# Two state-space groups in one block of a hybrid transformer kernel

## The chip, the cores and the metric

The kernel runs on one core of one Trainium2 chip. The metric is the device time of one execution in microseconds (us); the median of several runs counts. A core has five engines with their own instruction queues: TensorE (PE; its weight loads are shown apart as PEld), VectorE (DVE), ScalarE (ACT), GpSimd (POOL) and SyncE (SP), which here only starts transfers. Engines wait for each other by semaphores. TensorE writes its products to PSUM, which has eight banks of 128x512 fp32; everything else lives in SBUF. TensorE's clock has two levels, 1.2 and 2.4 GHz; the profile gives the granted clock as a share of 2.4 GHz, and "cold" and "warm" below mean the lower and the higher one.

## What is computed

A block with a hybrid mixer and a mixture of experts, then two more layers with attention. The change touches the state-space (SSD) part of the first mixer: 16 heads of width 64 in two groups of 8, for 512 tokens in both directions. For one direction of one group:

```python
c = silu(centred_dwconv(n @ w_in, conv_w, conv_b))     # B, C, x of the group; z is a gate
cs = cumsum(dt * A)                                    # per head, within a chunk
Lmat = exp(cs_i - cs_j), j <= i
y_intra = ((C_i . B_j) * Lmat) @ (x * dt)
chunk_states = B^T @ (x * dt * exp(cs_last - cs))
h = h * exp(cs_last) + chunk_states                    # carried from chunk to chunk
y = y_intra + (C @ h) * exp(cs)
y = (y_fw + y_bw + D * x) * silu(z)
y = rms_norm(y over the 512 channels of the group)
```

The kernel uses chunks of 128 tokens, four of them.

## The kernel before

The program is a row of stages. `stage` (line 63) opens a block in which each engine has its own instruction list, and ends it with a barrier of all engines that also clears the semaphores. Activations lie with channels on the 128 partitions and the 512 tokens in the free dimension, so a "tile" is 128 channels x 512 tokens. All products are fp32.

The mixer first normalizes its input to `m.xT` (8 tiles), then runs one long stage `gdn` (line 754) for the other kind of heads, four pairs of them. That stage also projects and convolves the ten tiles of SSD group 0 at its end (`ssd_order`): tiles 0 and 1 are B and C, 2 to 5 are x, 6 to 9 the gates z. Then `ssd_group` (line 1252) is called for g = 0 and 1. For group 1 it begins with the stage of `mixer_tiles` (line 661): five slabs of weights (1 MB each, four buffers of `m.ring`), ten tiles of 8 multiplications each (`product`, line 104), six of them through the seven taps of `convolve` (lines 650 and 654 on VectorE, two tiles in turns) and a SiLU on ScalarE (line 702), four directly through a SiLU (line 705). The other four stages run for each group:

- `ssd_tokens` (line 1280): TensorE transposes B and the x tiles (1287) and multiplies C with B (1290); VectorE scales the transposed x by step sizes into `x_in` and `x_out` (1306) and masks the C-B product (1310).
- `ssd_states` (line 1313): six multiplications (1321), and on VectorE the carried states (1333, 1336, 1339).
- `ssd_heads` (line 1342): 16 combinations of head pair j, head hh and direction d. GpSimd lays out `gu` (1352, two buffers), TensorE makes two 128x512 products of it (1364, 1365) in banks 0 to 3, ScalarE takes their exponentials (1396) into `c_dec` and `score`, and VectorE multiplies these with C (1413) and with the masked C-B (1416). Combination n waits until the exponentials of n - 2 have freed its banks. After each four combinations TensorE makes an output tile of 28 short products (1385), which VectorE adds to D x (1405) and multiplies with the gate (1409).
- `ssd_norm` (line 1422): squares on ScalarE (1430), four products with ones (1438), mean, root (1432), reciprocal (1447) and four products with the gain (1449).

So the two groups take nine stages. Nothing of group 1 starts before group 0 is done. The part behind it, `down_stage`, multiplies with `w_out`.

## Time and profile before

| | us |
|---|---|
| median of 3 runs (3831.04 to 3834.41) | 3832.28 |
| profiled execution | 3832.88 |
| its span | 3831.0 |
| TensorE busy in the span | 3380.7 |
| VectorE / ScalarE / GpSimd busy | 1742.8 / 1030.6 / 246.7 |
| mean granted clock | 0.937 |
| the state-space stages, first transposes of group 0 to last product of norm 1 | 768.2 to 1023.8 |

The page gives sums over the whole program, of which the state-space stages are 7%. To read them one needs the timeline of each engine in 767 to 1024 us, and the busy times by stretch. In a row of the timeline the first number is the start, the second the time from the first start to the last end of the merged instructions (an instruction's own time overlaps the next a little), "x16" their count, and the bracket the idle time of the engine before it and what ended it. "PEq L67" is the barrier.

### The profile page before, as it was taken

Reading aid. Unit: us, or ns where it says so; the run is one execution under the profiler, and the core shown is the slowest. Engines: PE = TensorE matmul, PEld = TensorE weight load, DVE = VectorE, ACT = ScalarE, POOL = GpSimd, SP = SyncE. Lnnn points to the kernel's source line nnn. Section 1 sums busy time; section 2 is a strip of 40 time slices with the busy share of each in tenths; the row PEclk is TensorE's granted clock in tenths of the full one; section 3 lists DMA queues with packets and bytes.
Section 4 is the critical chain, followed back from the end, with each engine's and each line's share of the span. In section 5 each row is a group of like instructions: output and inputs, shape, how many; then the busy total and the mean of one; then the engine's idle time right before and its main releaser. Section 6 shows DMA issues by size and latency. Waiting matters only on the chain. (4 is left out here: it accounts for less than half of the span.)

```text
span 3831.0 us, 39352 instructions
## 1 busy us (share of the span) xinstructions
PE 3380.7 (88%) x15418; PEld 2434.6 (64%) x15418; DVE 1742.8 (45%) x2515; ACT 1030.6 (27%) x1467; POOL 246.7 (6%) x212
## 2 busy tenths in 40 slices
PE   4988899868877775999998889998999998889997
PEld 3464765633465223788784557887888784468886
DVE  2757676664533002543235645432543326644433
ACT  2121211220321002322213443222322213543222
POOL 1100100020210001000002000000000002000001
PEclk6999999979887998999998899999999999899998
DMA  2100010001212992322211013221322211013221
GB/s 76 56 34 34 12 45 33 1 12 44 77 58 87 420 420 94 121 99 95 89 69 61 1 45 121 99 97 63 117 91 95 102 52 61 1 66 110 99 99 55
DMA packets 50693, 326.33 MB, mean 85 GB/s; under 512 B 7041, under 2 KB 7425, under 8 KB 13057
## 3 DMA queue, kind: packets, MB, share of 16 engines
q1 hardware_dynamic: 50560, 324.52, 22.7%
q8 instruction: 89, 1.46, 0.2%
q14 instruction: 44, 0.35, 0.0%
HBM read 321.35 MB, written 2.10 MB: 84 GB/s over the span
## 5 line engine op out<-in xcount | busy, mean ns | idle before, releaser
L364 PE MATMUL psum<-ffn_x_hi,ffn_w_hi 128*128 128x512 f32 x1408 | 548.8, 390 | 1.1 <-DVE ffn_x_lo L320 1.0
L364 PE MATMUL psum<-ffn_x_lo,ffn_w_hi 128*128 128x512 f32 x1408 | 547.8, 389 | 0.0
L364 PE MATMUL psum<-ffn_x_hi,ffn_w_lo 128*128 128x512 f32 x1408 | 547.8, 389 | 0.0
L309 DVE TENSOR_TENSOR ffn_w_lo<-ffn_raw,ffn_w_hi 128x2048 fp32r<-128x2048 f32 x128 | 293.4, 2292 | 420.6 <-ACT ffn_w_hi L280 420.6
L104 PE MATMUL psum<-mix_normed,mix_ring 128*128 128x512 f32 x832 | 378.9, 618 | 51.3 <-DVE recurrences_work L654 21.5
L280 ACT ACTIVATE ffn_w_hi<-ffn_raw 128x2048 fp32r<-128x2048 f32 x128 | 245.2, 1916 | 566.9 <-PE psum L364 566.8
L104 PEld LDWEIGHTS psum<-mix_normed,mix_ring 128*128 128x128 f32 x832 | 164.1, 199 | 262.6 <-issue 238.5
L364 PEld LDWEIGHTS psum<-ffn_x_hi,ffn_w_hi 128*128 128x128 f32 x1408 | 264.6, 188 | 61.1 <-DVE ffn_w_lo L316 6.5
L364 PEld LDWEIGHTS psum<-ffn_x_lo,ffn_w_hi 128*128 128x128 f32 x1408 | 264.7, 188 | 55.0
L364 PEld LDWEIGHTS psum<-ffn_x_hi,ffn_w_lo 128*128 128x128 f32 x1408 | 264.3, 188 | 54.9
L364 PE MATMUL psum<-ffn_hid_hi,ffn_w_hi 128*128 (+1 forms) x704 | 273.9, 389 | 0.0
L364 PE MATMUL psum<-ffn_hid_lo,ffn_w_hi 128*128 (+1 forms) x704 | 273.9, 389 | 0.0
L364 PE MATMUL psum<-ffn_hid_hi,ffn_w_lo 128*128 (+1 forms) x704 | 273.9, 389 | 0.0
L335 DVE TENSOR_TENSOR ffn_lift<-psum,squares_sb 128x512 f32<-128x512 f32 x88 | 60.8, 691 | 309.8 <-PE psum L364 309.8
L364 PEld LDWEIGHTS psum<-ffn_hid_hi,ffn_w_hi 128*128 128x128 f32 x704 | 132.1, 188 | 27.5
L364 PEld LDWEIGHTS psum<-ffn_hid_lo,ffn_w_hi 128*128 128x128 f32 x704 | 132.1, 188 | 27.4
L364 PEld LDWEIGHTS psum<-ffn_hid_hi,ffn_w_lo 128*128 128x128 f32 x704 | 132.1, 188 | 27.4
L654 DVE SCALAR_TENSOR_TENSOR recurrences_work<-psum,mix_group_cols,recurrences_work 128x509 f32<-128x509 f32 (+2 forms) x216 | 143.3, 745 | 0.0
L172 POOL TENSOR_TENSOR squares_sb<-squares_sb,ffn_gates 128x512 f32<-128x512 f32 x28 | 35.9, 1283 | 1451.4 <-ACT ffn_gates L162 1447.9
L298 ACT ACTIVATE ffn_hid_hi<-ffn_lift 128x512 f32 (+1 forms) x88 | 55.6, 632 | 267.7 <-DVE ffn_lift L339 267.7
L416 PE MATMUL psum<-mix_out_s_hi,mix_out_w_hi 128*128 128x512 f32 x256 | 101.0, 395 | 7.1 <-DVE mix_out_w_lo L473 7.1
L172 POOL TENSOR_TENSOR squares_sb<-squares_sb,mix_norm_tmp 128x512 f32<-128x512 f32 x42 | 53.6, 1276 | 826.1 <-ACT mix_norm_tmp L162 820.9
(454 smaller groups left out, 5323.3 us busy)
## 6 DMA issues: line engine op xcount, KB each, us to landing
ffn_raw<-w_ffn SPq DMA_DIRECT2D x128, 1024.0 KB, 4.7
mix_ring<-w_experts SPq DMA_DIRECT2D x48, 1024.0 KB, 13.6
mix_ring<-w_mix SPq DMA_DIRECT2D x32, 1024.0 KB, 7.0
mix_normed<-w_experts SPq DMA_DIRECT2D x24, 1024.0 KB, 13.6
experts_slabs<-w_experts SPq DMA_DIRECT2D x24, 1024.0 KB, 13.6
mix_ring<-w_gdn SPq DMA_DIRECT2D x16, 1024.0 KB, 4.8
mix_ring<-w_ssd SPq DMA_DIRECT2D x10, 1024.0 KB, 4.8
mix_ring<-w_out SPq DMA_DIRECT2D x7, 1024.0 KB, 7.1
```

Source lines behind the costliest of these rows:

```text
L104: ins = pe.matmul(out, weights(k), moving(k), start=(k == 0), stop=(k == n - 1))
L172: pool.tensor_tensor(m.squares, m.squares, tmp[:, k % 2, :], ALU.add).then_inc(folded, 1)
L280: act.activation(w_hi[:, q, :], raw[:, q, :], ACT.Copy).then_inc(hi_done, 1)
L298: act.activation(hid_hi[:, n, :], lift, ACT.Copy).then_inc(hid_hi_done, 1)
L309: dve.tensor_tensor(w_lo[:, q, :], raw[:, q, :], w_hi[:, q, :].bitcast(F32), ALU.subtract)\
L335: dve.tensor_tensor(lift, m.ps[:, 2 * q + 1, :], rstd, ALU.mult).then_inc(taken, 1)
L364: ins = pe.matmul(out, wp[:, q, w], xp, start=start and a == 0, stop=stop and a == 2)
L416: pe.matmul(out, a[0], b[0], start=start, stop=False)
L654: ins = dve.scalar_tensor_tensor(d[:, lo:hi], s[:, lo + shift:hi + shift], col[:, tap:tap + 1], d[:, lo:hi], ALU.mult, ALU.add)
```

## The change

`ssd_group`, `mixer_tiles` and the loop over the groups give way to one function `ssd_groups` with one stage for both groups. Each engine's list is now one written order:

- SyncE asks for the five slabs of group 1 at the start, into two buffers (the second half of the ring); slab s waits until the tiles of s - 2 are projected.
- TensorE puts the tiles of group 1 in pairs (`tiles(s)`, in the order 6, 7, 0, 1, 2, 3, 4, 5, 8, 9, in banks 6 and 7) between the steps of group 0, and the tokens, states and norm sums of either group between heads.
- VectorE convolves a pair (`conv`) between the products of the heads of group 0; ScalarE's SiLUs stand between its exponentials.
- Norm 0's squares, sums, mean, root and products stand among the heads of group 1.
- Buffers move: group 1 has its own tiles `c[1]`, its columns are in `m.cur_buf`, `score[0]` is where `x_out` was, the squares replace the gates, and `y` replaces the x tiles. Banks are given out by `token_banks` and `state_banks`.

The computation and the number of products are the same.

The core of the diff:

```diff
-        return [cut(m.work, (6 + i) * T, T) for i in range(4)]
+        return [m.mixed[:, KD + 6 + i, :] for i in range(2)] + [cut(m.rope_tables, i * T, T) for i in range(2)]
...
-def ssd_group(nc, m, io, g):
+def ssd_groups(nc, m, io):
...
-        mixer_tiles(nc, m, f"ssd_project_{g}", io["w_ssd"], g, io["ssd_cols"][g], 6, 4, c, gate)
+    scal = lambda n, g: m.scal[n][:, :, :, (0 if n == "step_to_end" else GH) + 8 * g:][:, :, :, 0:8]
+    combos = [(j, hh, d) for j in range(4) for hh in range(2) for d in range(2)]
...
+    place = {n: at for at, n in enumerate(order)}
+    tile_bank = lambda n: m.ps[:, 6 + place[n] % 2, :]
+    token_banks = ((0, 1, 2, 3, 4, 5), (4, 5, 6, 7, 4, 5))
+    state_banks = ((0, 1, 2, 3, 4, 5), (6, 7, 4, 5, 6, 7))
+    flat = lambda a: a.rearrange("p t i -> p (t i)")
...
-    with stage(nc, m, f"ssd_tokens_{g}") as (block, sem):
...
+    with stage(nc, m, "ssd") as (block, sem):
...
+        @block.sync
+        def _(sp):
+            sp.dma_start(cols[1], io["ssd_cols"][1]).then_inc(cols_in, 16)
+            for s in range(len(order) // 2):
+                if s >= 2:
+                    sp.wait_ge(projected, 2 * (s - 1))
+                sp.dma_start(slab(s).rearrange("p k n -> p (k n)"),
+                             io["w_ssd"][len(order) // 2 + order[2 * s] // 2]).then_inc(landed[s % 2], 16)
+
...
+            def tiles(s):
+                pe.wait_ge(landed[s % 2], 16 * (s // 2 + 1))
+                for at in (2 * s, 2 * s + 1):
+                    if s == 1:
+                        pe.wait_ge(silued, at - 1)
+                    elif s:
+                        pe.wait_ge(steps, 14 * (s - 1))
+                    product(pe, m.ps[:, 6 + at % 2, :], lambda k: slab(s)[:, k, at % 2 * P:at % 2 * P + P],
+                            lambda k: m.xT[:, k, :]).then_inc(projected, 1)
...
+            def tokens(g):
+                banks = token_banks[g]
+                if g:
+                    pe.wait_ge(y_read, 4)
+                    pe.wait_ge(silued, len(order))
+                for p, n in enumerate((0, 2, 3, 4, 5)):
...
-    with stage(nc, m, f"ssd_states_{g}") as (block, sem):
...
-    with stage(nc, m, f"ssd_heads_{g}") as (block, sem):
...
-    with stage(nc, m, f"ssd_norm_{g}") as (block, sem):
...
+            def fresh_states(g):
+                pe.wait_ge(b_copied, g + 1)
+                pe.wait_ge(taken, 4 * g + 4)
+                pe.wait_ge(cross_read, g + 1)
...
+                            pe.wait_ge(state_done, 6 + at - 3)
+                        pe.matmul(m.ps[:, state_banks[g][at], :], b_tok[:, t, :], x_out[:, d, t, :], start=True,
+                                  stop=True).then_inc(fresh, 1)
...
+            def decay(g, n):
+                d, at = n % 2, 16 * g + n
+                pe.wait_ge(laid, at + 1)
+                if at >= 2:
+                    pe.wait_ge(decayed, 2 * (at - 1))
+                else:
+                    pe.wait_ge(state_done, 6)
+                pe.matmul(m.ps[:, 2 * (n % 2), :], m.ones, flat(gu[:, n % 2, :, :]), start=True, stop=True)\
+                    .then_inc(decays, 1)
+                pe.matmul(m.ps[:, 2 * (n % 2) + 1, :], after[d], flat(gu[:, n % 2, :, :]), start=True, stop=True)\
+                    .then_inc(decays, 1)
+
+            def outputs(g, i):
+                if 4 * g + i >= 2:
+                    pe.wait_ge(y_read, 4 * g + i - 1)
+                if i < 2:
+                    pe.wait_ge(state_done, 6 * g + 6)
+                pe.wait_ge(scored, 32 * g + 2 * (4 * i + 4))
...
+            def sums(g):
+                if g == 0:
+                    pe.wait_ge(state_done, 11)
+                for i in range(4):
+                    pe.wait_ge(squared, 4 * g + i + 1)
+                    ins = pe.matmul(m.ps[:, 6, :], m.ones, gate[g][i], start=(i == 0), stop=(i == 3))
+                ins.then_inc(summed, 1)
+
+            tokens(0)
+            tiles(0)
+            fresh_states(0)
+            tiles(1)
+            for n in range(4):
+                decay(0, n)
+            for j in range(1, 5):
+                for n in range(4 * j, 4 * j + 4) if j < 4 else ():
+                    decay(0, n)
+                if j < 4:
+                    tiles(j + 1)
+                outputs(0, j - 1)
+            decay(1, 0)
+            decay(1, 1)
+            tokens(1)
+            decay(1, 2)
+            decay(1, 3)
+            fresh_states(1)
+            sums(0)
+            for j in range(1, 5):
+                for n in range(4 * j, 4 * j + 4) if j < 4 else ():
+                    decay(1, n)
+                outputs(1, j - 1)
+            sums(1)
...
+            def silu(n):
+                act.wait_ge(projected, place[n] + 1)
+                if n < 6:
+                    act.wait_ge(steps, 14 * (n // 2 + 1))
+                    act.activation(c[1][:, n, :], c[1][:, n, :], ACT.Silu).then_inc(silued, 1)
+                else:
+                    act.activation(gate[1][n - 6], tile_bank(n), ACT.Silu).then_inc(silued, 1)
...
+            def exps(g, ns):
+                for n in ns:
+                    if n >= 8:
+                        act.wait_ge(y_done, 4 * g + n // 4 - 1)
+                    elif g:
+                        act.wait_ge(y_done, 3 + n // 4)
+                    for half, dst in ((0, c_dec), (1, score[g])):
+                        act.wait_ge(decays, 32 * g + 2 * n + half + 1)
+                        act.activation(dst[:, n % 8, :], m.ps[:, 2 * (n % 2) + half, :], ACT.Exp).then_inc(decayed, 1)
...
+            copy_b(0)
+            for n in (6, 7, 0, 1):
+                silu(n)
+            exps(0, range(0, 8))
+            for n in (2, 3):
+                silu(n)
+            exps(0, range(8, 12))
+            for n in (4, 5):
+                silu(n)
+            exps(0, range(12, 16))
+            for n in (8, 9):
+                silu(n)
+            exps(1, range(0, 2))
+            copy_b(1)
+            squares(0)
+            exps(1, range(2, 8))
+            root(0)
+            exps(1, range(8, 16))
+            squares(1)
+            root(1)
...
+            def conv(a):
+                two = (a, a + 1)
+                if a == 0:
+                    dve.wait_ge(cols_in, 16)
+                convolve(dve, m, [tile_bank(n) for n in two], [c[1][:, n, :] for n in two],
+                         [cols[1][:, 8 * n:8 * n + 8] for n in two], projected, [place[n] + 1 for n in two], steps,
+                         7 * a)
+
...
+            tokens(0)
+            carry(0)
+            conv(0)
+            scores(0, range(0, 8))
+            conv(2)
+            out(0, 0)
+            scores(0, range(8, 12))
+            conv(4)
+            out(0, 1)
+            scores(0, range(12, 16))
+            out(0, 2)
+            out(0, 3)
+            tokens(1)
+            carry(1)
+            scores(1, range(0, 4))
+            average(0)
+            scores(1, range(4, 8))
+            normed(0)
+            out(1, 0)
+            scores(1, range(8, 12))
+            out(1, 1)
+            scores(1, range(12, 16))
+            out(1, 2)
+            out(1, 3)
+            average(1)
+            normed(1)
 
 
 
@@ -3034,8 +3110,7 @@
                     resid_norm_stage(nc, m, "norm1", m.gains["norm1"], m.xT)
                     scalars_stage(nc, m, io)
                     gdn_heads(nc, m, io)
-                    for g in range(SG):
-                        ssd_group(nc, m, io, g)
+                    ssd_groups(nc, m, io)
                 down_stage(nc, m, "mix1_out", io["w_out_1"], 0, m.mixed, 2 * KD, 1.0)
             resid_norm_stage(nc, m, "norm2", m.gains["norm2"], m.xT)
             with expert_memory(nc, m):
```

What moves on TensorE, at the start of the state-space part. Line 1287 (now 1280) are the transposes, 1321 (1298) the state products, 104 the projection tiles; branches stand where a stage ends. Before:

```order
L1287 MATMUL psum<-const_sb,recurrences_work 128x128 x20
L1290 MATMUL psum<-recurrences_work 128x128 x4
L65 UNCONDITIONAL_BRANCH
L1316 UNCONDITIONAL_BRANCH
L1321 MATMUL psum<-recurrences_work 128x512 x6
L65 UNCONDITIONAL_BRANCH
L1355 UNCONDITIONAL_BRANCH
```

After:

```order
L1259 UNCONDITIONAL_BRANCH
L1280 MATMUL psum<-const_sb,recurrences_work 128x128 x20
L1285 MATMUL psum<-recurrences_work 128x128 x4
L104 MATMUL psum<-mix_normed,mix_ring 128x512 x16
L1298 MATMUL psum<-recurrences_work 128x512 x6
L104 MATMUL psum<-mix_normed,mix_ring 128x512 x16
L1308 MATMUL psum<-mix_norm_tmp,const_sb 128x512
L1310 MATMUL psum<-mix_norm_tmp,const_sb 128x512
```

Two pairs of tiles of group 1 now stand ahead of and behind the state products, and no stage ends between them.

What moves on ScalarE, in the heads of group 0 (line 1396, now 1392, are the exponentials; 1296/1374 the copy of B; 702/1380 SiLUs of convolved tiles and 705/1382 of gates; 1430 and 1432 belong to norm 0). Before:

```order
L1296 ACTIVATE recurrences_work<-psum 128x512
L65 UNCONDITIONAL_BRANCH
L1389 UNCONDITIONAL_BRANCH
L1396 ACT_TABLE_LOAD
L1396 ACTIVATE mix_ring<-psum 128x512 x32
L65 UNCONDITIONAL_BRANCH
L1427 UNCONDITIONAL_BRANCH
L1430 ACTIVATE mix_ring<-recurrences_work 128x512 x4
L1432 ACT_TABLE_LOAD
```

After (the two exponentials of combination 0 are shown, of the 16 ahead of the next SiLU):

```order
L1374 ACTIVATE recurrences_work<-psum 128x512
L1382 ACT_TABLE_LOAD
L1382 ACTIVATE mix_mixed<-psum 128x512 x2
L1380 ACTIVATE recurrences_work<-recurrences_work 128x512 x2
L1392 ACT_TABLE_LOAD
L1392 ACTIVATE mix_ring<-psum 128x512
L1392 ACTIVATE recurrences_work<-psum 128x512
```

The SiLUs of four tiles of group 1 now stand ahead of the first exponential of group 0, and table loads come between SiLUs and exponentials.

## Rows read from the trace of the kernel before

**Rows 1.** The head of the page: span and instruction count.

```profile
span 3831.0 us, 39352 instructions
```

**Rows 2.** Stretches: length, busy us of PE, PEld, DVE, ACT, POOL; PEclk, DMA share, GB/s.

```profile
857.00:935.00 78.00, 71.93 (x160) 31.40 (x160) 28.30 (x42) 6.64 (x11) 0.00 (x0) 0.92 0.18 68
...
767.00:1024.00 257.00, 197.61 (x832) 100.56 (x832) 150.61 (x191) 57.18 (x91) 39.38 (x32) 0.85 0.05 21
```

**Rows 3.** Timeline (start us, us, engine, line, operation [idle before]): where norm 0 ends and projection 1 starts.

```profile
853.85 2.74 DVE L1449 SCALAR_TENSOR_TENSOR mix_mixed<-recurrences_work,mix_group_cols,mix_norm_tmp 128x512 f32<-128x512 f32 x4
...
857.50 1.28 ACT L702 ACT_TABLE_LOAD   x1 [7.08 <-PEq L67]
...
857.87 22.28 SPq L675 DMA_DIRECT2D mix_ring<-w_ssd  x5
...
862.79 71.93 PE L104 MATMUL psum<-mix_normed,mix_ring 128*128 128x512 f32 x160 [13.76 <-DMA mix_ring<-w_ssd]
```

**Rows 4.** Timeline, TensorE, state-space stages (a 128x512 f32 multiplication is two records).

```profile
768.21 4.50 PE L1287 MATMUL psum<-const_sb,recurrences_work 128*128 128x128 f32 x20 [11.25 <-PEq L67]
...
782.00 7.84 PE L1321 MATMUL psum<-recurrences_work 128*128 128x512 f32 x12 [8.06 <-PEq L67]
...
804.95 1.02 PE L1364 MATMUL psum<-mix_norm_tmp,const_sb 128*128 128x512 f32 x2
...
812.07 3.28 PE L1385 MATMUL psum<-mix_ring,recurrences_work 128*64 128x128 f32 x56
...
842.36 6.68 PE L1438 MATMUL psum<-mix_ring,const_sb 128*128 128x512 f32 x8 [3.14 <-ACT mix_ring L1430]
...
936.30 2.38 PE L1287 MATMUL psum<-const_sb,recurrences_work 128*128 128x128 f32 x20 [1.58 <-PEq L67]
```

**Rows 5.** Timeline, VectorE, state-space stages.

```profile
770.19 9.66 DVE L1306 TENSOR_TENSOR recurrences_work<-psum,mix_scalars 128x512 f32<-128x512 f32 x16 [2.96 <-PE psum L1287]
...
779.76 1.28 DVE L1310 TENSOR_TENSOR recurrences_work<-psum,const_sb 128x512 f32<-128x512 f32 x2
...
803.55 1.53 DVE L1413 TENSOR_TENSOR mix_ring<-mix_ring,recurrences_work 128x512 f32<-128x512 f32 x1
...
815.89 0.73 DVE L1405 SCALAR_TENSOR_TENSOR recurrences_work<-recurrences_work,mix_group_cols,psum 128x512 f32<-128x512 f32 x1
...
840.05 0.69 DVE L1409 TENSOR_TENSOR recurrences_work<-recurrences_work,mix_mixed 128x512 f32<-128x512 f32 x1
...
850.46 3.35 DVE L1447 RECIPROCAL mix_norm_tmp<-mix_norm_tmp 128x512 f32<-128x512 f32 x1 [0.69 <-ACT mix_norm_tmp L1432]
...
893.57 0.81 DVE L650 TENSOR_SCALAR recurrences_work<-psum,mix_group_cols 128x512 f32<-128x512 f32 x1 [4.33 <-PE psum L104]
...
907.30 0.81 DVE L650 TENSOR_SCALAR recurrences_work<-psum,mix_group_cols 128x512 f32<-128x512 f32 x1 [4.33 <-PE psum L104]
...
908.02 7.96 DVE L654 SCALAR_TENSOR_TENSOR recurrences_work<-psum,mix_group_cols,recurrences_work 128x509 f32<-128x509 f32 x12
...
1021.09 2.74 DVE L1449 SCALAR_TENSOR_TENSOR mix_mixed<-recurrences_work,mix_group_cols,mix_norm_tmp 128x512 f32<-128x512 f32 x4
```

**Rows 6.** Timeline, ScalarE: an exponential, a table load and what follows it.

```profile
699.52 1.28 ACT L973 ACT_TABLE_LOAD   x1
...
700.82 1.15 ACT L973 ACTIVATE mix_mixed<-mix_mixed 128x512 f32<-128x512 f32 x2
...
797.52 0.60 ACT L1396 ACTIVATE mix_ring<-psum 128x512 f32<-128x512 f32 x1 [1.95 <-PE psum L1364]
```

**Rows 7.** Timeline, GpSimd: one cumulative decay tile.

```profile
803.47 1.06 POOL L1352 TENSOR_TENSOR mix_norm_tmp<-const_sb,mix_scalars 128x512 f32<-128x512 f32 x1 [0.39 <-PE psum L1365]
```

**Rows 8.** TensorE after idle time: a timeline row, then stretches as in rows 2.

```profile
681.89 16.98 PE L104 MATMUL psum<-mix_normed,mix_ring 128*128 128x512 f32 x32 [3.47 <-DVE recurrences_work L654]
...
795.00:800.00 5.00, 4.59 (x6) 2.01 (x7) 0.83 (x2) 1.76 (x3) 2.09 (x3) 0.50 0.00 2
...
800.00:805.00 5.00, 5.00 (x13) 2.04 (x12) 4.23 (x4) 2.98 (x5) 2.70 (x3) 0.94 0.00 0
```

292 lines of the change are left out of this document (111 added, 181 removed).

## The prediction

> **What bounds the kernel now.** I read the busy time by stretch first. The state-space part runs from 767 to 1024 us of a span of 3831.0 us [rows 1, 2]. TensorE is busy 197.61 of these 257 us, more than any other engine, but at a mean granted clock of 0.85 of the full 2.4 GHz: part of its busy time is the same work at 1.2 instead of 2.4 GHz. So the part is a chain that goes through TensorE, with stops at the stage ends. I then read the timeline at one such end. The last product of norm 0 ends at 853.85 + 2.74 = 856.59, the next stage's first instruction starts at 857.50, so a barrier costs 0.9 us. Behind it the first weight slab is asked for at 857.87, and TensorE starts at 862.79, 4.9 us later, after 13.76 us idle [rows 3]. All of projection 1 (71.93 us of TensorE) stands alone: VectorE is busy 28.30 of 78 us there [rows 2, 3]. The token and norm stages are the opposite: VectorE or a short chain works, and TensorE waits.
>
> **Times of the parts.** Twenty transposes take 2.38 us warm and 4.50 us cold [rows 4]. Two projection tiles of 8 multiplications took 907.30 - 893.57 = 13.73 us [rows 5], so one 128x512 multiplication takes 0.86 us warm, and a cold one 1.7 (6.68 us for four, [rows 4]). A combination (head, direction) has two of them, 1.72 us. An output tile takes 3.28 less overlap, 3.2. On VectorE the scaling of the tokens and the C-B product take 9.66 + 1.28 - overlap = 10.9 us, a convolution of two tiles 0.7 + 7.96 = 8.7 us after the second tile is there [rows 5]. On ScalarE two SiLUs take about 1.15, a table load 1.28, an exponential 0.60 [rows 6].
>
> **The walk after the change.** It starts at the same point, 768.2 [rows 4]; all before it is unchanged.
> (1) Transposes and cross products of group 0 as before, to 774.0. The first slab is now asked for at the same barrier and needs the same 4.9 us, to about 773: hidden. The next two tiles end at 787.8. Group 0's scaling on VectorE (until 781.0, [rows 5]) lies under them.
> (2) Six state multiplications 5.1, then tiles 3 and 4 13.7: 806.6. The carried states are under those tiles.
> (3) Here is the new wait. Combinations 0 and 1 fill the two pairs of PSUM banks, until 810.0. Combination 2 needs the exponentials of 0, and on ScalarE these stand behind the SiLUs of tiles 0 and 1 (the order of ScalarE above, lines 1380 and 1392), which need the convolution of both. Convolution 0.2 + 8.7, SiLUs 1.2, table 1.3, two exponentials 1.2: 12.5 us after the tile pair, 819.1. TensorE idles 9.1 us.
> (4) Six combinations 10.3, two tiles 13.7: 843.1. After such an idle stretch the clock is low: after 3.47 us idle, 32 records (two tiles) took 16.98 us where 13.73 is warm [rows 5, 8]. After the states ended at 782.00 + 7.84 = 789.8, TensorE came back at about 795.4 (busy 4.59 of the stretch 795 to 800), ran at 0.50 there and at 0.94 in the next 5 us [rows 4, 8]. That is 2.3 (half of 4.6) to 3.2 us each; I take 2.7. Sum 845.8.
> (5) Then twice the same period from tile pair to tile pair: 12.5 to the freed banks (outputs of 3.2 and two combinations of 3.4 fill it up to a gap of 5.8 us), two combinations 3.4, cold clock 2.7, tiles 13.7, together 32.3: 878.1 and 910.4.
> (6) Two output tiles 6.4, combinations 0 and 1 of group 1 3.4, the transposes up to VectorE's first tile 1.9, its scaling 10.9 (combinations 2 and 3 under it): 933.0. TensorE has been idle 4 us.
> (7) Six state multiplications 5.1 + 2.7 cold, waiting for the carried states 0.7, sums of norm 0 3.4: 944.9.
> (8) From combination 4 to the last gating before: 804.95 to 840.05 + 0.69 = 840.74, 35.8 us. VectorE sets the pace there: it takes eight combinations from 798.1 (797.52 + 0.60, [rows 6]) to 815.89, 2.2 us each against TensorE's 1.72; one of its two products is stretched to 1.53 us while GpSimd makes a decay tile [rows 5, 7]. So norm 0's work there (0.69 mean, 3.35 reciprocal, 2.74 products) adds up to 6.8 [rows 5], at least 0 if it fills holes. I take 5.9, near the upper end since that engine is the late one: 986.6.
> (9) The last norm: square 0.6, one sum multiplication (three are done already) 1.7, mean 0.7, root 0.7, reciprocal 3.4, products 2.7, handovers 0.3: 996.7. Before, this tail took 856.59 - 840.74 = 15.9 in group 0.
>
> Before, the same place is 1021.09 + 2.74 = 1023.8 [rows 5]. The gain is 27.1 us by this sum. Handovers of 0.05 to 0.2 us between engines, some ten more on the chain than I listed, take back about 1: **26 us**. The profiled execution took 3832.88 us, 1.88 around its span, and the median is 0.6 lower. 3832.3 - 26 gives **3806 us** (the like of 3806.9 for a profiled one).
>
> Two edits cost nothing. The barriers: eight are gone, about 7.5 us, already in the walk since it has none. The slab loads: two buffers instead of four, but a slab has 25 us and more between its uses and takes 4.9.
>
> A rule that speaks against the change. A table load is 1.28 us, and the next ScalarE instruction starts 0.02 us behind it (699.52 + 1.28 = 700.80, then 700.82) [rows 6]. The new order of the two groups has 11 loads where 5 stood, but only the three of steps 3 to 5 are on the chain. The Trainium skill, "ScalarE: Activation LUTs", section "Table sets: the hidden batching unit", says to do all functions of one set before switching, and "What ACT_TABLE_LOAD costs" gives 2.66 us a switch, since a drain comes on top. By that the three would cost 4.1 us more, and the result would be 3810. The rows show no such drain.
>
> **The rivals.**
> - Clock holds. If gaps of 4 to 6 us did not lower the clock, and that of 9 did not either, 4 x 2.7 = 10.8 us fall out: 3795. Rows 8 speak against it.
> - GpSimd stretches the convolutions too. While conv runs, TensorE consumes two decay tiles, so GpSimd makes two more; products with both inputs in SBUF were stretched by 1.53 - 0.69 = 0.84 [rows 5, 7]. No convolution of before runs beside GpSimd, so the bounds are 0 and 3 x 2 x 0.84 = 5.0 us: 3811. I take 0, because a convolution step has its main input in PSUM like the scaling steps, and only one in SBUF. The Trainium skill, "SBUF — State Buffer", section "Who interferes with whom", has the same condition: only a VectorE instruction with two SBUF inputs contends with a GpSimd one that reads SBUF. By that it is 0.
> - A switch of ScalarE costs as much again on the chain. By the nearest row, one more 1.28 us for each of the three: 3.8, so 3810. Rows 6, with 0.02 us behind a load, speak against it. This is the rule above.
> - The overlap doesn't come: the idle stretches are as long as what was hidden, and only barriers (7.5) and the wait for the slab (5.3) are saved: 3819.
> - Slower. If TensorE stayed at the low clock through the interleaved stretch (819 to 921), its 82 us of warm work there (three tile pairs 41, 16 combinations 27, four outputs 13) would grow. It turns slower where over 26 us of it, a third, run cold beyond the short restarts; wholly cold gives 3870. The gaps are 6 us in 32, and before, the clock was back at 0.94 within 5 us [rows 8], so 0.02.
>
> **How the numbers follow.** Forecast 0.70 (3801 to 3811), clock holds 0.08, GpSimd 0.07, drains 0.05, no overlap 0.06, within 0.2% of before 0.02, slower 0.02. A measurement can tell about 0.2%, 7.7 us, from no change. The range 3797 to 3816 takes in the forecast with its own bounds (step 4: 0.5 a gap; step 8: +0.9, -5.9), GpSimd and drains; it leaves out most of "clock holds", "no overlap" and the last two, 0.18. Faster 0.96, same 0.02, slower 0.02.
>
> **What would show it.** In the timeline of TensorE after the change: idle stretches of about 9, 6 and 6 us before combinations 2, 10 and 14 of group 0, each ended by a ScalarE exponential, and a clock of 0.5 behind them; transposes of group 1 near 921; the last product near 997. Twelve convolution steps in 8.0 us as before would rule out GpSimd's lock, a gap above 0.1 us between a load and its activation would show the drain. I am wrong above all if the stretch from combination 4 of group 1 isn't paced by VectorE, or if the gaps in step 5 are longer than 5.8 us.

## The result and the profile after

| | before | after |
|---|---|---|
| median of 4 runs, us | 3833.17 (3831.04 to 3834.41) | 3801.95 (3796.39 to 3804.26) |
| profiled execution / its span | 3832.88 / 3831.0 | 3804.26 / 3802.2 |
| state-space part, first transposes to last product of norm 1 | 768.21 to 1023.83: 255.6 | 772.78 to 999.00: 226.2 |

The ratio is 0.9918 (95% interval 0.9906 to 0.993): 31.2 us faster, against a forecast of 26 us (3806, range 3797 to 3816).

Outside the state-space part nothing changed: the rest of the span is 3831.0 - 255.6 = 3575.4 us before and 3802.2 - 226.2 = 3576.0 after. Over all kernels shown below this rest lies between 3567 and 3580 us from one profiled execution to the next, although its code is the same, so a difference of a few us is read from the length of the part, not from medians. The part itself repeats: a second profile of the changed kernel, in another set of runs, gave 226.2 us again.

The head of the page of the changed kernel, and the stretch that holds the part (length, busy us of PE, PEld, DVE, ACT, POOL, PEclk, DMA share, GB/s), answering [rows 1, 2]:

```profile
span 3802.2 us, 39200 instructions
...
772.00:1000.00 228.00, 188.17 (x833) 97.35 (x833) 139.92 (x190) 63.33 (x98) 37.56 (x32) 0.91 0.07 24
```

TensorE is busy 188.17 of 228 us at a mean clock of 0.91, where it was 197.61 of 257 at 0.85. The work is the same; its busy time is shorter because less of it runs cold.

TensorE's timeline after the change, answering [rows 3, 4]:

```profile
772.78 4.50 PE L1280 MATMUL psum<-const_sb,recurrences_work 128*128 128x128 f32 x20 [11.26 <-PEq L67]
778.71 14.00 PE L104 MATMUL psum<-mix_normed,mix_ring 128*128 128x512 f32 x32 [0.25 <-DMA mix_ring<-w_ssd]
...
792.54 5.31 PE L1298 MATMUL psum<-recurrences_work 128*128 128x512 f32 x12
797.69 13.90 PE L104 MATMUL psum<-mix_normed,mix_ring 128*128 128x512 f32 x32
811.43 1.02 PE L1308 MATMUL psum<-mix_norm_tmp,const_sb 128*128 128x512 f32 x2
...
824.10 2.05 PE L1308 MATMUL psum<-mix_norm_tmp,const_sb 128*128 128x512 f32 x2 [9.08 <-ACT recurrences_work L1392]
825.94 1.91 PE L1310 MATMUL psum<-mix_norm_tmp,const_sb 128*128 128x512 f32 x2
...
836.97 13.90 PE L104 MATMUL psum<-mix_normed,mix_ring 128*128 128x512 f32 x32
...
864.66 2.05 PE L1308 MATMUL psum<-mix_norm_tmp,const_sb 128*128 128x512 f32 x2 [6.95 <-ACT recurrences_work L1392]
...
870.77 13.90 PE L104 MATMUL psum<-mix_normed,mix_ring 128*128 128x512 f32 x32
...
898.46 2.04 PE L1308 MATMUL psum<-mix_norm_tmp,const_sb 128*128 128x512 f32 x2 [6.96 <-ACT recurrences_work L1392]
...
904.74 13.90 PE L104 MATMUL psum<-mix_normed,mix_ring 128*128 128x512 f32 x32
...
940.44 7.08 PE L1298 MATMUL psum<-recurrences_work 128*128 128x512 f32 x12 [3.87 <-DVE recurrences_work L1440]
...
951.81 1.02 PE L1308 MATMUL psum<-mix_norm_tmp,const_sb 128*128 128x512 f32 x2
...
984.54 3.28 PE L1331 MATMUL psum<-mix_ring,recurrences_work 128*64 128x128 f32 x56 [1.39 <-DVE mix_ring L1478]
```

The 13.76 us of idle time before the projection [rows 3] are 0.25 us now. In their place stand three idle stretches, 9.08, 6.95 and 6.96 us, each ended by a ScalarE exponential, and behind each of them products that take 2.05 and 1.91 us instead of 1.02. The state products of group 1, behind a wait of 3.87 us, run partly cold as well (7.08 us, where group 0's take 5.31). The clock rows behind the first of the three stretches show the lower of the two levels, 1.2 GHz, and then the way up (columns as above):

```profile
824.00:826.00 2.00, 1.90 (x3) 0.89 (x4) 2.00 (x4) 0.94 (x2) 0.00 (x0) 0.50 0.03 8
...
828.00:830.00 2.00, 2.00 (x4) 0.72 (x3) 1.02 (x2) 1.09 (x2) 0.98 (x1) 0.76 0.00 0
```

What ScalarE does before the first two of these stretches end (1382 and 1380 are SiLUs, 1392 exponentials):

```profile
774.52 1.28 ACT L1382 ACT_TABLE_LOAD   x1
...
820.41 1.15 ACT L1380 ACTIVATE recurrences_work<-recurrences_work 128x512 f32<-128x512 f32 x2 [27.07 <-DVE recurrences_work L654]
821.58 1.28 ACT L1392 ACT_TABLE_LOAD   x1
822.87 0.60 ACT L1392 ACTIVATE mix_ring<-psum 128x512 f32<-128x512 f32 x1
...
859.67 1.28 ACT L1380 ACT_TABLE_LOAD   x1 [21.91 <-DVE recurrences_work L654]
860.97 1.15 ACT L1380 ACTIVATE recurrences_work<-recurrences_work 128x512 f32<-128x512 f32 x2
862.13 1.28 ACT L1392 ACT_TABLE_LOAD   x1
863.43 0.60 ACT L1392 ACTIVATE mix_ring<-psum 128x512 f32<-128x512 f32 x1
```

TensorE has filled the two pairs of PSUM banks that the exponentials are to free, and ScalarE waits for the convolution of the next two tiles, because in its list their SiLUs stand first. In the second stretch there are two table loads in the chain, not one: the load for the SiLU starts only when the convolution is done. A load doesn't always wait for the work behind it. The first one, at 774.52, ran at once, and its SiLU waited for its tile until 785.88. The list has one wait in front of that SiLU, and two in front of those of line 1380. In this profile the loads ahead of a single wait that lasted (774.52, 905.55, 990.01) all ran ahead of it, and the loads that stood behind an idle stretch (859.67, 893.48, 926.03, 963.37) all belong to activations with two. No run changes this alone.

VectorE and GpSimd beside each other, a convolution with two decay tiles, and at the end the norms (VectorE rows 1495 and 1498):

```profile
812.36 7.96 DVE L654 SCALAR_TENSOR_TENSOR recurrences_work<-psum,mix_group_scalars,recurrences_work 128x509 f32<-128x509 f32 x12
...
813.39 1.05 POOL L1256 TENSOR_TENSOR mix_norm_tmp<-const_sb,mix_scalars 128x512 f32<-128x512 f32 x1 [38.57 <-PE psum L1310]
815.11 1.05 POOL L1256 TENSOR_TENSOR mix_norm_tmp<-const_sb,mix_scalars 128x512 f32<-128x512 f32 x1 [0.67 <-PE psum L1310]
...
962.51 3.34 DVE L1495 RECIPROCAL const_sb<-const_sb 128x512 f32<-128x512 f32 x1
965.88 4.32 DVE L1498 SCALAR_TENSOR_TENSOR mix_mixed<-recurrences_work,mix_group_cols,const_sb 128x512 f32<-128x512 f32 x4
...
988.63 0.69 DVE L1487 TENSOR_TENSOR recurrences_work<-recurrences_work,const_sb 128x512 f32<-128x512 f32 x1
...
996.26 2.74 DVE L1498 SCALAR_TENSOR_TENSOR mix_mixed<-recurrences_work,mix_group_scalars,const_sb 128x512 f32<-128x512 f32 x4
```

### The profile page after: what moved, and what is told of

It is laid out like the page before. It is cut to its first block and busy times, and to the rows that moved or that the text cites. A ratio compares the mean times of both kernels' runs of the same rounds, so it can differ in the third digit from the quotient of the medians.

```text
span 3802.2 us, 39200 instructions
## 1 busy us (share of the span) xinstructions
PE 3369.6 (89%) x15418; PEld 2427.8 (64%) x15418; DVE 1732.8 (46%) x2515; ACT 1037.4 (27%) x1473; POOL 244.7 (6%) x212
## 5 line engine op out<-in xcount | busy, mean ns | idle before, releaser
L172 POOL TENSOR_TENSOR squares_sb<-squares_sb,ffn_gates 128x512 f32<-128x512 f32 x28 | 35.9, 1282 | 1450.0 <-ACT ffn_gates L162 1446.6
L654 DVE SCALAR_TENSOR_TENSOR recurrences_work<-psum,mix_group_cols,recurrences_work 128x510 f32<-128x510 f32 (+2 forms) x180 | 119.4, 741 | 0.0
```

Source lines behind the costliest of these rows:

```text
L172: pool.tensor_tensor(m.squares, m.squares, tmp[:, k % 2, :], ALU.add).then_inc(folded, 1)
L654: ins = dve.scalar_tensor_tensor(d[:, lo:hi], s[:, lo + shift:hi + shift], col[:, tap:tap + 1], d[:, lo:hi], ALU.mult, ALU.add)
```

## The experiments

Each was compared with the kernel before on its own chip, whose medians there were 3831.14, 3831.51, 3832.03 and 3829.4 us. Line numbers in the diffs' kernels are those of the changed kernel, shifted by a few lines where code was added.

**Again.** The changed kernel itself.

> The changed kernel once more, beside the others of this set. It should come within 0.2% of its first median, 3802 us, and the state-space part (first transposes to last product of norm 1) should again take 226.2 us, since nothing in it depends on chance but the clock. If the 29.4 us of that part in the first profile were partly luck of the clock, the part would take 229 or more here.

Measured: 3799.77 us (3797.5 to 3802.73), ratio 0.9918 (0.9903 to 0.9934), part 226.2 us, as expected. It serves as the point of comparison below.

**Exponentials first.** Only ScalarE's list is reordered, so that each pair of SiLUs stands behind the exponentials that TensorE waits for.

```diff
-            for n in (6, 7, 0, 1):
+            for n in (6, 7):
                 silu(n)
             exps(0, range(0, 8))
-            for n in (2, 3):
+            for n in (0, 1):
                 silu(n)
             exps(0, range(8, 12))
-            for n in (4, 5):
+            for n in (2, 3):
                 silu(n)
             exps(0, range(12, 16))
-            for n in (8, 9):
+            for n in (4, 5, 8, 9):
                 silu(n)
```

> The changed kernel with ScalarE's list in another order: each batch of exponentials of group 0 stands ahead of the SiLUs of the tile pair in front of which TensorE waited (exponentials 0 to 7, then SiLUs 0 and 1, and so on). Nothing else is changed. Theory 'gaps': the three idle stretches of TensorE (9.1, 7.0 and 7.0 us) are due only to this order, so they go, and the cold restarts behind them (2.5 to 2.7 us each) go too: 23 + 8 = 31 us less, about 3771 us, part about 196 us. Rival 'VectorE takes over': the products wait for the same VectorE that convolves, so the gaps come back as waits for scored products, and no more than 10 us are gained: 3792 us or more.

Measured: 3777.75 us (3774.88 to 3784.16), ratio 0.9865 (0.985 to 0.988), part 204.8 us: 21.4 less, two thirds of the 31 us that theory 'gaps' expected and far more than the 10 of its rival. The three idle stretches are gone. But a new one of 6.60 us stands in the first group's heads. TensorE's row, then GpSimd's, then the first and the last of twelve VectorE products:

```profile
823.29 2.07 PE L1308 MATMUL psum<-mix_norm_tmp,const_sb 128*128 128x512 f32 x2 [6.60 <-POOL mix_norm_tmp L1256]
...
815.06 9.18 POOL L1256 TENSOR_TENSOR mix_norm_tmp<-const_sb,mix_scalars 128x512 f32<-128x512 f32 x2 [0.67 <-PE psum L1310]
...
815.04 0.68 DVE L1475 TENSOR_TENSOR mix_ring<-mix_ring,recurrences_work 128x512 f32<-128x512 f32 x1
...
821.66 0.68 DVE L1478 TENSOR_TENSOR recurrences_work<-recurrences_work 128x512 f32<-128x512 f32 x1
```

Two decay tiles took 9.18 us instead of 2.1. VectorE's products stand 0.60 us apart from 815.04 to 822.34, none of them stretched, and TensorE goes on 0.95 us behind the last of them, which is about one tile (1.05). So GpSimd was shut out for the whole run. The sum closes to 0.3 us: the three stretches are 23.0 us and their cold restarts 7.7 ("clock kept" below), less 6.60 and 1.9 for the new one (2.07 + 1.88 - 2.04) makes 22.2. The state products of group 1 were slower here, 8.46 us instead of 7.08, and from their start to the norm sums it took 1.1 us more, which leaves 21.1 against the measured 21.4.

The same happened once more in this run, for a shorter time, in the heads of group 1. GpSimd's row, then TensorE's:

```profile
948.30 4.06 POOL L1256 TENSOR_TENSOR mix_norm_tmp<-const_sb,mix_scalars 128x512 f32<-128x512 f32 x2 [3.67 <-PE psum L1310]
...
950.96 1.12 PE L1308 MATMUL psum<-mix_norm_tmp,const_sb 128*128 128x512 f32 x2 [1.02 <-POOL mix_norm_tmp L1256]
```

The first of these two tiles began 0.18 us behind the sixth of eight VectorE products (948.12). That one and the next two took their usual 0.68 us, and TensorE waited 1.02 us for the tile. In the changed kernel the tile at the same place, 974.78, began 0.18 us behind the sixth product too (974.60), and there it got its turn after that product: it took 1.40 us, and the next product was stretched to 1.53.

**Serial.** One block as in the change, but the projection isn't interleaved: group 0's heads, then ten tiles in a row through all eight banks, then group 1. Norm 0 still stands among the heads of group 1. All of ScalarE's exponentials of group 0 stand ahead of its SiLUs, all of VectorE's scores ahead of its convolutions.

```diff
-    order = (6, 7, 0, 1, 2, 3, 4, 5, 8, 9)
+    order = tuple(range(10))
...
-    tile_bank = lambda n: m.ps[:, 6 + place[n] % 2, :]
+    tile_bank = lambda n: m.ps[:, place[n] % 8, :]
...
-            tiles(0)
             fresh_states(0)
-            tiles(1)
...
-                if j < 4:
-                    tiles(j + 1)
                 outputs(0, j - 1)
+            for s in range(5):
+                tiles(s)
+            pe.wait_ge(silued, len(order))
```

> One block without barriers, but with no interleaving: group 0's heads are finished first, then the ten tiles of group 1 run in one row through eight PSUM banks, as before the change, then group 1. Theory 'gaps': interleaving in the written order pays for what it hides (23 us idle and 8 us cold clock against some 20 us of hidden token and state work); the gain of the change comes from the eight barriers (7.5), the wait for the first slab (5.3), the hidden norm 0 (12 to 16) and fewer cold restarts. Then this kernel is no slower than the changed one: the part takes 213 to 226 us, 3787 to 3802 us. Rival 'overlap': the projection beside the heads is what gains, and without it only barriers and slab wait remain: 3815 to 3819 us.

Measured: 3788.35 us (3778.89 to 3793.13), ratio 0.9886 (0.9871 to 0.99), part 209.5 us: 46.1 less than before and 16.7 less than the interleaved change, and even below the 213 to 226 of theory 'gaps'. TensorE's states of group 0, and the ten tiles:

```profile
785.18 8.19 PE L1300 MATMUL psum<-recurrences_work 128*128 128x512 f32 x12 [7.30 <-DVE recurrences_work L1433]
...
836.89 68.93 PE L104 MATMUL psum<-mix_normed,mix_ring 128*128 128x512 f32 x160
```

The tiles run warm without a stop, 68.93 us where the stage of before took 71.93 and had a wait of 6.2 ahead of it (862.79 - 856.59, [rows 3]). So the gain of the change doesn't come from hiding the projection. It comes from the single block with norm 0 in it, and the interleaving of the projection, in the order in which ScalarE's list has it, loses 16.7 us of that again. In the better order of "exponentials first" it gains 4.7 (204.8 against 209.5). By pieces, from rows of before and of this run: up to the first projection tile 64.7 us instead of 72.5 up to the last gating (7.8), norm 0 off the path (15.9), projection 68.9 instead of 79.7 up to the transposes of group 1 (10.8), and group 1 75.9 instead of 87.5 (11.6); together 46.1. These are differences of rows; no run takes out one of them alone.

**Two barriers.** The kernel before, with a second bare barrier at the end of each of the nine state-space stages.

```diff
+    if name.startswith('ssd_'):
+        nc.all_engine_barrier()
```

> The kernel before with a second barrier of all engines behind each of its nine state-space stages. Theory 'barrier is 0.9 us': 9 x 0.8 to 1.0 = 7 to 9 us more, about 3841 us. Rival 'a barrier also costs clock': the longer idle times lower TensorE's clock where it now holds, up to 2.7 us for some of them: 3845 to 3855 us.

Measured: 3831.69 us (3823.92 to 3841.23, 11 runs), ratio 1.0003 (0.9994 to 1.0013). No difference, where 3841 us or more was expected. TensorE's wait ahead of the states, which was 8.06 [rows 4]:

```profile
781.74 7.67 PE L1323 MATMUL psum<-recurrences_work 128*128 128x512 f32 x12 [8.40 <-PEq L69]
```

It grew by 0.34 us, and the like waits of group 1 by 0.33 (9.97 against 9.64, 1.91 against 1.58). A bare barrier behind another one thus costs a third of the 0.9 us that passed at a stage end [rows 3]. The rest of the 0.9 (branches, the clearing of semaphores, the wait for each engine's last instruction) wasn't taken apart. Nine times 0.33 is 3.0 us, less than the runs can tell. In this profile the part was even 2.2 us shorter than in that of before, 253.4, mainly because the sums of norm 1 took 3.70 us where [rows 4] has 6.68 for the like of norm 0: a cold or warm restart at one and the same place differs between executions.

**Clock kept.** The change, with 10, 7 and 7 multiplications on constants in the three idle stretches, into banks that are free there (VectorE's reading of an output tile is waited for before the last). Each takes 0.87 us warm (two records).

```diff
-            for n in range(4):
-                decay(0, n)
+            decay(0, 0)
+            decay(0, 1)
+            keep_running(pe, m, m.ps[:, 4, :], 10)
+            decay(0, 2)
+            decay(0, 3)
...
+                    if n in (10, 14):
+                        if n == 14:
+                            pe.wait_ge(y_read, 1)
+                        keep_running(pe, m, m.ps[:, 5 if n == 10 else 4, :], 7)
```

> The changed kernel with idle work in TensorE's three gaps: 10, 7 and 7 multiplications with no use, into a bank that is free, ahead of combinations 2, 10 and 14 of group 0 (8.6, 6.0 and 6.0 us in gaps of 9.08, 6.95 and 6.96). Theory 'the gap is paid twice': the restart behind each gap is cold and costs 2.3 to 2.9 us more, and the work keeps the clock, so the part shrinks from 226.2 by 7 to 8 us, to about 219; median about 3793. Rival: the clock is not what makes the first combinations behind a gap slow (ScalarE and VectorE pace them, the banks come free late): no change, 226.

Measured: 3790.91 us (3788.46 to 3791.32), ratio 0.9892 (0.9875 to 0.9908), part 219.2 us. The first stretch now, filled with 20 records, and the product behind it:

```profile
809.08 8.75 PE L111 MATMUL psum<-const_sb 128*128 128x512 f32 x20
818.32 1.10 PE L1308 MATMUL psum<-mix_norm_tmp,const_sb 128*128 128x512 f32 x2 [0.50 <-ACT recurrences_work L1399]
...
828.83 13.90 PE L104 MATMUL psum<-mix_normed,mix_ring 128*128 128x512 f32 x32
...
926.92 8.33 PE L1298 MATMUL psum<-recurrences_work 128*128 128x512 f32 x12 [3.87 <-DVE recurrences_work L1447]
```

The product takes 1.10 us and not 2.05. The part is 226.2 - 219.2 = 7.0 us shorter, as the theory has it, and the stretches themselves remain: ScalarE is as late as before. The price of each restart is read from the rows, from the first product behind the stretch to the next tile pair: 828.83 - 818.32 = 10.51 us, where the change has 836.97 - 824.10 = 12.87, so 2.4 us; at the other two stretches 3.51 us each, where the change has 6.11 and 6.28, so 2.6 and 2.8. Together that is 7.7. Of this 1.1 was lost again at the state products of group 1, which take 8.33 us here and 7.08 in the change, behind the same wait of 3.87 us (the granted clock is 0.50 from their start here; in the change it is 0.90 for their first 2 us and 0.50 only after that), and 0.4 was gained at the first tiles, which didn't wait for their slab here.

**Without norm 0 on VectorE.** Its mean (1491) stays, and so does the root on ScalarE.

```diff
-                dve.wait_ge(inverted, g + 1)
+                dve.wait_ge(inverted, 1)
...
-            normed(0)
+            dve.wait_ge(rooted, 1)
```

> The changed kernel without VectorE's reciprocal and four products of norm 0 (6.1 us of work, 7.6 as they ran beside GpSimd); the output of these four tiles is left out. My sum gave 5.9 us to norm 0 among the heads of group 1, since VectorE was to be the late engine there: then the part falls to 220.5. Rival 'it fills holes': the only wait for a VectorE product there is 1.39 us, in front of the last output tile, so the part falls by about 1.4, to 224.8.

Measured: 3798.0 us (3790.76 to 3806.19), ratio 0.9903 (0.9886 to 0.9921), part 224.5 us: only 1.7 less, as the rival has it. From combination 4 to the last gating the time is 35.9 us (950.94 to 986.81), with norm 0 37.5 (951.81 to 989.32). VectorE's rows where norm 0 was:

```profile
961.63 0.73 DVE L1484 SCALAR_TENSOR_TENSOR recurrences_work<-recurrences_work,mix_group_scalars,psum 128x512 f32<-128x512 f32 x1
962.40 0.69 DVE L1487 TENSOR_TENSOR recurrences_work<-recurrences_work,mix_mixed 128x512 f32<-128x512 f32 x1
964.41 0.69 DVE L1475 TENSOR_TENSOR mix_ring<-mix_ring,recurrences_work 128x512 f32<-128x512 f32 x1 [1.32 <-ACT mix_ring L1392]
```

VectorE comes to the output tile at once and then waits 1.32 us for ScalarE's exponentials; behind that, more of its products meet a decay tile and are stretched. Its waits from there to the last gating add up to 5.1 us, and to 2.1 with norm 0. So the five instructions, 7.7 us as they ran beside GpSimd (3.34 + 4.32), mostly filled time in which VectorE would have waited, or in which its products would have been stretched. The price of the whole norm 0 wasn't measured: the wait of 1.32 us holds a table load of ScalarE (962.49, 1.28 us) which the root makes necessary, and which this version keeps.

**GpSimd let in.** "Exponentials first", and VectorE waits before the products of combination n until GpSimd has laid three tiles more.

```diff
             def scores(g, ns):
                 for n in ns:
                     d = n % 2
+                    if g == 0:
+                        dve.wait_ge(laid, n + 3)
```

> e1_exps_first with one more wait on VectorE: the products of combination n of group 0 wait until GpSimd has laid the tile of n + 2. In e1_exps_first VectorE ran 12 products back to back behind the convolution, GpSimd's two tiles took 9.18 us instead of 2.1, and TensorE idled 6.60 us and came back cold. Theory 'lock': GpSimd gets in only when VectorE makes a pause, so the wait removes that gap and its cold restart, 8 to 9 us: part 196, median about 3769. Rival: GpSimd was late for another reason, or the pauses cost VectorE as much: part 204.8 as without the wait, 3778.

Measured: 3779.27 us (3776.04 to 3785.85), ratio 0.9864 (0.9846 to 0.9882), part 202.1 us: 2.7 less than without the waits, not the gain expected. GpSimd's row, and the VectorE product behind the first wait that held:

```profile
819.72 6.78 POOL L1256 TENSOR_TENSOR mix_norm_tmp<-const_sb,mix_scalars 128x512 f32<-128x512 f32 x2 [0.67 <-PE psum L1310]
...
825.53 1.52 DVE L1477 TENSOR_TENSOR mix_ring<-mix_ring,recurrences_work 128x512 f32<-128x512 f32 x1 [0.94 <-POOL mix_norm_tmp L1256]
```

The waits came too late by their own numbers: combinations 0 to 3 need only six tiles, so eight products ran on before VectorE stopped. What they show all the same: VectorE stopped at 824.59, and the tile that VectorE waited for ended 0.94 us later. TensorE waited 4.19 us instead of 6.60.

**Filled.** The same, and four multiplications on constants before the states of group 1, where TensorE waited 3.87 us.

```diff
+            pe.wait_ge(taken, 6)
+            keep_running(pe, m, m.ps[:, 6, :], 4)
             fresh_states(1)
```

> e6_let_pool_in with four multiplications of no use in TensorE's wait for the scaled tokens of group 1 (3.87 us), ahead of the state products. Expected from the clock: state products and norm sums there stay at the full clock, 2.5 to 3 us less than e6_let_pool_in, part about 193.5, median 3766. Rival: VectorE's carried states pace that stretch, and nothing is gained.

Measured: 3776.59 us (3771.98 to 3780.17), ratio 0.9854 (0.9837 to 0.9871), part 199.8 us, 2.3 less, where 2.5 to 3 were expected. The states of group 1 (8.29 us in the run before, 7.08 in the change):

```profile
910.77 5.39 PE L1298 MATMUL psum<-recurrences_work 128*128 128x512 f32 x12 [0.43 <-DVE recurrences_work L1442]
```

From their start to that of the norm sums the time is 6.71 us, in the run before 8.95. So this cold restart, behind 3.87 us of idle time, cost 2.2 us and is gone; GpSimd was shut out as in the run before (6.78 us for two tiles).

**All tiles laid first.** The same, but VectorE waits once, ahead of its first product, for eight tiles.

```diff
-                    if g == 0:
-                        dve.wait_ge(laid, n + 3)
+                    if g == 0 and n == 0:
+                        dve.wait_ge(laid, 8)
```

> The version with the fill before the second group's states, with one edit: VectorE waits once, before the first of the 32 products of the first group, until GpSimd has laid eight tiles, and not before each combination for three tiles more. In the run before this one GpSimd's sixth tile began at the same time as the first product (within 0.02 us), two tiles took 6.8 us instead of 2.1, and TensorE waited 4.19 us for them, cold behind it (2.08 and 1.53 us where 1.02 is usual): the wait there first held VectorE back after eight products. Theory: GpSimd gets no turn while VectorE's products stand back to back; with the wait ahead of them the 4.19 us and about 1.6 us of the cold restart go, so the state-space part falls from 199.8 to about 194 us and the median from 3776.6 to about 3771. Rival: the two tiles are slow for another reason (ScalarE's exponentials or TensorE's reads beside them); then they take 6.8 us with VectorE still, TensorE's wait stays at 4 us, and VectorE's products, begun some 7 us later, end 5 us later and push the convolutions behind them: part 200 to 205 us, median 3777 to 3782.

Measured: 3769.01 us (3763.49 to 3773.76, 5 runs), ratio 0.9833 (0.9819 to 0.9847), part 194.2 us: 5.6 less, as expected, and with "shifted" below the fastest version: 63 us below the kernel before. TensorE has no idle stretch left in the heads of group 0. But the theory as it was put there doesn't hold. GpSimd's ninth and tenth tile (counted from the first), and the VectorE product between them:

```profile
818.54 1.57 POOL L1256 TENSOR_TENSOR mix_norm_tmp<-const_sb,mix_scalars 128x512 f32<-128x512 f32 x1 [0.67 <-PE psum L1310]
820.26 1.30 POOL L1256 TENSOR_TENSOR mix_norm_tmp<-const_sb,mix_scalars 128x512 f32<-128x512 f32 x1 [0.15 <-PE psum L1310]
...
819.12 1.53 DVE L1479 TENSOR_TENSOR mix_ring<-mix_ring,recurrences_work 128x512 f32<-128x512 f32 x1
```

Products stand back to back here too, and each tile got its turn after at most one of them (1.57 and 1.30 us instead of 1.05); the next product was stretched to 1.53 as in [rows 5]. Being back to back alone doesn't shut GpSimd out.

**Shifted.** "Filled" without VectorE's waits; a copy of 16 columns onto themselves ahead of the products, so that their run starts later but has no pause.

```diff
-                    if g == 0:
-                        dve.wait_ge(laid, n + 3)
+                    if g == 0 and n == 0:
+                        dve.wait_ge(steps, 14)
+                        dve.tensor_copy(cols[1][:, 0:16], cols[1][:, 0:16])
```

> The version with the fill before the second group's states, with VectorE's waits for GpSimd's tiles taken out again, and one small thing in their place: before the first of its 16 products behind the first convolution VectorE waits for its own last convolution step and copies 16 columns onto themselves. That moves the run of products by 0.1 to 0.3 us and puts no pause into it. Open is what makes GpSimd lose its turn in two runs (a tile that began 0.02 us behind the first product waited for 12 and for 8 of them), while elsewhere, and with the products held back until eight tiles were laid, a tile that met back-to-back products got its turn after one (tiles of 1.3 to 1.6 us instead of 1.05). Theory: it is the coincidence of the two starts; shifted, no tile takes over 1.6 us, TensorE's wait of 4.2 us (6.6 without any wait on VectorE) is gone, the state-space part takes about 194 us and the median is about 3769. Rival: it comes from products standing straight behind the convolution; then the sixth tile is shut out again for the whole run of 12 products, TensorE waits some 6.6 us, part about 202 us, median about 3777.

Measured: 3770.94 us (3765.85 to 3774.74), ratio 0.9844 (0.9828 to 0.9861), part 194.4 us, as the theory has it.

```profile
815.38 0.99 DVE L1478 COPY mix_group_scalars<-mix_group_scalars 128x16 f32<-128x16 f32 x1
816.29 0.68 DVE L1480 TENSOR_TENSOR mix_ring<-mix_ring,recurrences_work 128x512 f32<-128x512 f32 x1
...
817.01 1.47 POOL L1256 TENSOR_TENSOR mix_norm_tmp<-const_sb,mix_scalars 128x512 f32<-128x512 f32 x1 [0.67 <-PE psum L1310]
```

The copy itself met a tile and took 0.99 us, so the run of products began some 0.9 us later, more than meant. With nothing but that, no tile in the heads of group 0 took over 1.5 us and TensorE didn't wait there. That the products stand without a pause is therefore not enough for the long wait. Whether the convolution straight ahead of them matters isn't shown, since the copy stands between; the shorter case of "exponentials first" had none ahead of it. In all three runs that had the long wait, the tile began 0.02 us behind the first product of the run (815.06 behind 815.04; 819.72 behind 819.70; the same in "filled"). But in "all tiles laid first" a tile began 0.02 us behind the second product (818.54 behind 818.52) and got its turn, and the shorter case began 0.18 us behind a sixth product, as did a tile of the changed kernel that got its turn. So the start of the tile against that of the product, to the 0.01 us that the rows give, doesn't decide it. What does stays open.

## Why the prediction was right, and where its sizes were off

The walk stands against the profile as follows; measured lengths are differences of the starts in the rows above (where a step ends with two tiles and no row follows them at once, their end is taken as start + 13.73).

| step | predicted us | measured us |
|---|---|---|
| 1 transposes, tiles 1 and 2 | 19.6 | 19.8 |
| 2 states, tiles 3 and 4 | 18.8 | 18.9 |
| 3 to combination 2 (idle 9.1) | 12.5 | 12.7 (9.08) |
| 4 six combinations, two tiles, cold | 26.7 | 26.6 |
| 5 two periods (idle 5.8) | 64.6 | 67.8 (6.95, 6.96) |
| 6 outputs, transposes, scaling | 22.6 | 22.0 |
| 7 states and sums | 11.9 | 11.4 |
| 8 combination 4 to last gating | 41.7 | 37.5 |
| 9 last norm | 10.1 | 9.7 |
| sum | 228.5 | 226.2 |

- **The sum.** It came out near the measured part partly by luck: step 5 was 3.2 us too small and step 8 was 4.2 us too large, and the two nearly cancel.
- **What bounds it, the slab, the barriers.** Right. The chain goes through TensorE, the first slab is hidden (0.25 us), and the stops at the stage ends are gone. The 0.9 us for a stage end is right as a distance in [rows 3] (eight of them are 7.3 us, a little less than the 7.5 of the prediction), but the runs don't show it to be a price of the barrier: a bare one costs 0.33.
- **Step 3, the new wait.** Right in place, releaser and size. "Exponentials first" removed it by an edit on ScalarE's list alone.
- **Step 4, cold restarts.** The mechanism is right, and so is the size: 2.7 was predicted, and by "clock kept" it is 2.4, 2.6 and 2.8.
- **Step 5.** Too small by 3.2 us. The failing term is "12.5 us" from the tile pair to the freed banks, taken over from step 3; it is 13.96 (850.70 to 864.66). In step 3 ScalarE has the SiLU table loaded beforehand; in step 5 the load for the SiLU stands in the chain as well (859.67, 1.28 us), once in each period. That is 2 x 1.46 of the 3.2; the rest are tenths at the restarts and handovers. The prediction counted eleven loads and put three on the chain; five are there.
- **The rule on table switches.** The trace shows no drain: the exponential starts 0.01 us behind its load (821.58 + 1.28, then 822.87), so the cost of a switch here is 1.28 us. The Trainium skill, "ScalarE: Activation LUTs", section "What ACT_TABLE_LOAD costs", has 2.66 us; the measurement decides. The same page's section "Table sets: the hidden batching unit" advises to keep functions of one set together. Here that would have helped, but less for the loads than for the order: the costly thing was that a SiLU waited in front of exponentials that were ready to run.
- **Step 8.** Too large by 4.2 us, and this is the largest error. The 35.8 us carried over from before hold (35.9 in "without norm 0"). The failing term is that for norm 0: 5.9, of which 1.7 are left when its reciprocal and products are taken out (the mean of 0.69 stays in). It was taken near its upper end "since that engine is the late one"; but VectorE isn't late for the whole stretch. Before norm 0 it had run through the scores of four combinations at 0.60 us a product, none of them stretched, and without norm 0 it waits for exponentials and for output tiles.
- **The rival "GpSimd stretches the convolutions".** Refuted: 12 convolution steps take 7.96 us with two decay tiles of 1.05 beside them, as in [rows 5] without. The Trainium skill, "SBUF — State Buffer", section "Who interferes with whom", has it so, and the trace agrees.
- **The rival "no overlap", 3819.** It fell in a way that the prediction missed. It held that without overlap only barriers and the slab wait are saved, 12.8 us. The serial version saves 46.1 in the part. The prediction had worked out all pieces of this (norm 0 hidden, combinations under transposes and scaling, no cold start of the projection), but put them into the interleaved sum and left them out of the rival. So the sum was right, and the picture behind it, that interleaving the projection is what pays, was wrong: as ordered it costs 16.7 us more than it brings.
- **The other rivals.** "Clock holds" and "slower" fell: products behind the idle stretches run at the lower level, and the clock is back at the higher one within two combinations each time (the fourth product takes 1.02, 1.03 and 1.19 us).
- **The sum against the median.** The part gained 29.4 us where 26 were forecast: 2.3 from the steps above, and 1 because the allowance for handovers wasn't needed. The median gained 31.2; the remaining 1.8 is within the scatter of the rest of the program.

## What to carry to other kernels

When a serial stage is cut up and put between the steps of another, write down for each engine what stands directly in front of the instruction that frees the bottleneck's buffers. Work that must wait for something late (here SiLUs behind a convolution) belongs behind the ready work that others wait for; here this order alone was worth 22 us. And price the version with the stages merged but not interleaved: it may already hold the gain.

## What the runs showed of the hardware

- GpSimd was shut out for 7.2 us by twelve VectorE products with both inputs in SBUF, back to back (two tiles in 9.18 us instead of 2.1); usually a tile waits for one product, some 0.3 to 0.5 us. The Trainium skill, "SBUF — State Buffer", section "Who interferes with whom", says that such a pair contends by an exclusive lock held for a whole instruction, and the stretched products and tiles agree with it. That VectorE got its turn twelve times in a row, and eight times in two other runs, is what the runs here show. In one run a second, shorter case held a tile back for three products. A start later by 0.9 us made the long one vanish; the condition is open.
- An idle stretch of 7 to 9 us of TensorE cost 2.4 to 2.8 us more behind it through the clock, and one of 3.9 us cost 2.2; multiplications on constants in it gave just these back.
- ScalarE's table load ran ahead of the wait of its activation where there was one wait, and behind the waits where there were two. In step 5 its 1.28 us stood on the chain so, although ScalarE had been idle for 21.91 us. That the number of waits is the cause wasn't tested.
- A second barrier right behind one costs 0.33 us.
